# Reordering a block-triangular inverse in a recurrent layer: products formed at eviction, and one product pair moved a stage earlier

## The chip, the core and the metric

The kernel runs on one NeuronCore of one Trainium2 chip, as one program with float32 inputs and outputs. The metric is the device time in microseconds (us). The core has TensorE (PE, with its weight loads shown as PEld), VectorE (DVE), ScalarE (ACT), GpSimd (POOL) and SyncE (SP), which run side by side and meet at semaphores.

## The reference

A batch of 256 tokens of width 1024 goes through two blocks. The first has two layers; each layer is an MLP, a mixing stage, a cross attention to 256 memory tokens and a second MLP. The second block has a gated recurrence, a differential attention and a mixture of experts. The part that this case touches is the recurrent half of the mixing stage, with 8 heads of width 64. Per head and token it does

```
sa    = state @ (-kk_t)
state = state * w_t + outer(sa, b_t) + outer(v_t, k_t)
y_t   = state @ r_t
```

with `kk` normalised per head, `b = kk * a`, and a decay `w` per channel. After it come a norm per head, a bonus term and a gate. The cross attention then reads `rms_norm(mem)`, the memory tokens scaled by their inverse root mean square and by a gain.

## The kernel before

Every stage is a block of the program in which each engine has its own list, written out by hand, and all engines meet at a barrier at the end of each stage. Large matrix products stream weights from HBM in 1 MB chunks through a ring of five slots (SP issues them). ACT rounds each chunk (L264), DVE subtracts the rounded part (L274), and TensorE multiplies in three passes (L289 to L291).

`mix_in_stage` computes the projections, a local attention and the operands of the recurrence. Its last DVE instructions on those operands are L993 to L998: L998 makes the removal operand `a` (which lives in `b.removal`). After that DVE and ACT still mix the last projected columns (L905, L1009, L914) while TensorE ends with the last attention value product (L844).

`rwkv_stage` (L1111), called once per layer, does the recurrence in chunks of 64 tokens. There are four chunks, held as two token tiles t = 0, 1 of 128 partitions with two chunks each (`cp`), and eight heads `e`. Each pair of chunk and head is a 64 x 64 problem on one quadrant of the TensorE array (rows by the partition half of the operands, columns by the half of the result). A float32 product is recorded as two weight loads and two matmuls. The work, in TensorE's order:

- gate product L1358 into banks 6 and 7; then the chunk products L1369: 32 with the removal operand `Bb` into banks 0 to 3, and 32 with the key operand `Kb` into banks 4 to 7. DVE makes `Kb` (L1228) and masks all of them into `chunk_products`, called `m4` (L1232 for removal, L1244 for keys). ACT evicts the gate (L1321).
- The inverse X of a unit lower triangular matrix is built by doubling in six levels. POOL masks the part A of level `lv` (L1295, two instructions a level, one per token tile, into two buffers `AL`). Level 0 is L1401 and L1404, evicted by DVE as I minus the product (L1237 to L1239).
- Levels 1 to 5 each do: A X on TensorE (`level_ax`, L1412) -> ACT copies it to G (L1334) -> X^T G (L1421) and G^T X^T (L1426) -> DVE subtracts them from X (L1252) and from X^T (L1255). X and X^T are both kept, since each is the weight operand of one product. L1412 and L1421 use all four quadrants; L1426 uses two. Level 5 needs only X^T.
- Between A X and the updates, TensorE has filler work: transposes of v (level 1), of the read operand (2), of `Bb` (3), the product `bv` (L1435, level 4) and the transposes of `Kb` (5), evicted by ACT (L1328, L1340).
- The tail: X applied to the right sides (L1462, evicted negated by ACT L1346 and DVE L1258), then products that build state and read matrices (L1475, L1480, L1484, L1488), outputs (L1495, L1499), two state steps (L1517), the reads from the states (L1508) and the bonus sum (L1527).
- As soon as L1462 is done, POOL loads the 1 MB of memory tokens into `h` (L1306), waits for them, and scales them in two halves (L1311, L1313) for the next stage.

`memory_stage` follows the barrier and starts with ACT L264 and L2251.

## Time and profile before

| what | value |
|---|---|
| median of 3 runs | 2081.26 us (2078.82 to 2083.69) |
| the profiled execution's own time | 2080.44 us |
| its span in the profile | 2078.6 us |
| PE busy | 1991.8 us, 96% of the span |
| `rwkv_stage`, first layer | 329.3 to about 396.2 us |
| `rwkv_stage`, second layer | 1038.6 to about 1102.7 us |

The profiled execution took 1.8 us more than its span, and 0.8 us less than the median. The page gives busy time per engine; a timeline row is start, duration, engine, source line, operation, result<-operands, shape and count, with the idle time before it and what ended it in brackets.

### The profile page before, as it was taken

How to read it: one execution, taken by the hardware profiler on the slowest of the kernel's cores; microseconds unless marked ns; L12 is line 12 of the kernel's file. 1: busy time of each engine (PE TensorE's matmuls, PEld its weight loads, DVE VectorE, ACT ScalarE, POOL GpSimd, SP SyncE). 2: the span in 40 equal slices, each digit the busy share in tenths (PEclk: the TensorE clock that was granted, in tenths of full speed). 3: DMA queues.
4: the chain of work that ended last, by engine and by line, in shares of the span. 5: the costliest groups of instructions: out<-in, count | busy, mean ns of one | idle time of the engine just before them, and what ended most of it. 6: DMA issues, size and time to landing. Idle time of an engine off the chain costs nothing. (4 is left out here: it accounts for less than half of the span.)

```text
span 2078.6 us, 34505 instructions
## 1 busy us (share of the span) xinstructions
PE 1991.8 (96%) x14152; PEld 1734.2 (83%) x14152; DVE 1434.1 (69%) x1856; ACT 1084.2 (52%) x1639; POOL 346.1 (17%) x193
## 2 busy tenths in 40 slices
PE   6999998899999999999989999998999989999999
PEld 5888887799888878889878998887899987888887
DVE  5784765566677567656645756765686658999997
ACT  5444662454544454446524544444565547777775
POOL 1660004200065026400051003620000000000000
PEclk9999999999999999999999999998999989999999
DMA  9654430253565456534204536654433317999995
GB/s 361 255 223 170 147 117 3 87 186 136 222 237 209 142 216 248 211 144 160 75 24 145 181 114 251 243 191 101 163 122 122 133 67 293 368 372 371 371 372 192
DMA packets 56247, 402.47 MB, mean 194 GB/s; under 512 B 6360, under 2 KB 6544, under 8 KB 7840
## 3 DMA queue, kind: packets, MB, share of 16 engines
q1 hardware_dynamic: 51216, 368.64, 47.2%
q0 software_dynamic: 4880, 31.68, 4.5%
q8 instruction: 112, 1.84, 0.4%
q14 instruction: 39, 0.32, 0.0%
HBM read 399.23 MB, written 1.06 MB: 193 GB/s over the span
## 5 line engine op out<-in xcount | busy, mean ns | idle before, releaser
L274 DVE TENSOR_TENSOR weights_lo<-ring,weights_hi 128x1024 fp32r<-128x1024 f32 x696 | 928.6, 1377 | 178.5 <-ACT weights_hi L264 178.1
L264 ACT CAST weights_hi<-ring 128x1024 fp32r<-128x1024 f32 x696 | 694.6, 1050 | 247.4 <-PE ps L291 218.0
L289 PE MATMUL ps<-weights_hi,act_hi 128*128 128x512 f32 (+1 forms) x960 | 358.4, 373 | 22.2 <-DVE weights_lo L274 17.1
L290 PE MATMUL ps<-weights_lo,act_hi 128*128 128x512 f32 (+1 forms) x960 | 351.9, 367 | 0.0
L291 PE MATMUL ps<-weights_hi,act_lo 128*128 128x512 f32 (+1 forms) x960 | 351.7, 366 | 0.0
L289 PE MATMUL ps<-act_hi,weights_hi 128*128 128x256 f32 x992 | 295.7, 298 | 11.9 <-DVE act_lo L2340 6.3
L290 PE MATMUL ps<-act_lo,weights_hi 128*128 128x256 f32 x992 | 287.5, 290 | 0.0
L291 PE MATMUL ps<-act_hi,weights_lo 128*128 128x256 f32 x992 | 287.1, 289 | 0.0
L289 PEld LDWEIGHTS ps<-weights_hi,act_hi 128*128 128x128 f32 x960 | 182.1, 190 | 54.5 <-DVE weights_lo L274 17.1
L289 PEld LDWEIGHTS ps<-act_hi,weights_hi 128*128 128x128 f32 x992 | 196.9, 198 | 17.9 <-issue 10.3
L291 PEld LDWEIGHTS ps<-weights_hi,act_lo 128*128 128x128 f32 x960 | 182.0, 190 | 32.6
L290 PEld LDWEIGHTS ps<-weights_lo,act_hi 128*128 128x128 f32 x960 | 182.3, 190 | 30.0
L290 PEld LDWEIGHTS ps<-act_lo,weights_hi 128*128 128x128 f32 x992 | 197.4, 199 | 0.1
L291 PEld LDWEIGHTS ps<-act_hi,weights_lo 128*128 128x128 f32 x992 | 196.7, 198 | 0.0
L289 PE MATMUL ps<-weights_hi,slot_hi 128*128 128x512 f32 x320 | 128.3, 401 | 0.9 <-DVE weights_lo L274 0.9
L291 PE MATMUL ps<-weights_hi,slot_lo 128*128 128x512 f32 x320 | 125.4, 392 | 0.0
L289 PE MATMUL ps<-weights_hi,mlp_hidden_hi 128*128 128x512 f32 x320 | 125.3, 392 | 0.0
L291 PE MATMUL ps<-weights_hi,mlp_hidden_lo 128*128 128x512 f32 x320 | 125.0, 391 | 0.0
L290 PE MATMUL ps<-weights_lo,slot_hi 128*128 128x512 f32 x320 | 124.9, 390 | 0.0
L662 POOL TENSOR_TENSOR stretch<-stretch,params 128x2048 f32<-128x2048 f32 x24 | 86.5, 3603 | 230.0 <-PE ps L291 230.0
L290 PE MATMUL ps<-weights_lo,mlp_hidden_hi 128*128 128x512 f32 x320 | 124.4, 389 | 0.0
L460 ACT ACTIVATE stretch<-ps,norm_rs 128x256 f32<-128x256 f32 x88 | 37.0, 471 | 133.3 <-PE ps L291 133.3
(535 smaller groups left out, 3098.3 us busy)
## 6 DMA issues: line engine op xcount, KB each, us to landing
ring<-stream SPq DMA_DIRECT2D x348, 1024.0 KB, 4.9
stretch<-ada_in POOLq DMA_DIRECT2D x24, 1024.0 KB, 5.4
h<-mem_in POOLq DMA_DIRECT2D x2, 1024.0 KB, 5.2
consts<-w_consts SPq DMA_DIRECT2D x1, 1376.0 KB, 7.7
x<-x_in SPq DMA_DIRECT2D x1, 1024.0 KB, 4.9
stretch<-mem_in POOLq DMA_DIRECT2D x1, 1024.0 KB, 10.1
bias_t<-bias_scratch POOLq DMA_DIRECT2D x1, 1024.0 KB, 6.8
out<-x SPq DMA_DIRECT2D x4, 256.0 KB, 2.1
```

Source lines behind the costliest of these rows:

```text
L264: core.nc.scalar.copy(self.hi[:, self.place(i), part], core.slot(chunk)[:, part]).then_inc(self.rounded.sem, 1)
L274: core.nc.vector.tensor_tensor(self.lo[:, self.place(i), part], core.slot(chunk)[:, part], self.hi[:, self.place(i), part].bitcast(F32), A ...
L289: nc.tensor.matmul(out, lhs[0], rhs[0], start=start, stop=False, **kw)
L290: nc.tensor.matmul(out, lhs[0], rhs[1], start=False, stop=False, **kw)
L291: return nc.tensor.matmul(out, lhs[1], rhs[0], start=False, stop=stop, **kw)
L460: nc.scalar.activation(sg[:, j % 2, t, :], inner_bank(j, t)[:, 0:STEP], ACT.Silu, scale=acts.rs[:, t:t + 1]).then_inc(silu.sem, 1)
L662: nc.gpsimd.tensor_tensor(w, w, c.unsqueeze(2).to_broadcast([P, KB, STEP]), ALU.mult).then_inc(self.added.sem, 1)
```

## The change

Only the recurrence and what feeds it are changed; the mathematics is the same.

- The 32 removal products move from the start of `rwkv_stage` to the end of TensorE's list in `mix_in_stage`. They wait for L998 (`removed`) and go to banks 2, 3, 6 and 7. The core's first DVE work is now their masking.
- G is no longer A X but I - A X: DVE forms it when it evicts the bank (`factor`), in place of ACT's copy. With that G, both updates are plain products, X G and its transpose, and are copied out, not subtracted from the old X. ACT copies X of tile 0 and the whole of X^T (both tiles, two banks, one instruction; only tile 0 in level 5), DVE copies X of tile 1 (and X^T of tile 1 in level 5).
- The turned update goes to all four quadrants: the layout of G and X^T over banks and halves changes with the level (`crosses`, `factor_place`, `end_place`).
- TensorE's list in a level is now A X of tile 0, filler, A X of tile 1, filler, then the X updates, then both turned updates. The fillers are: the key products in levels 1 and 2, the read transposes in 3, the `Bb` transposes in 4, `bv` in 5. The transposes of v go ahead of level 0 (banks 4, 5), and those of `Kb` between level 5 and the product with the right sides.
- POOL masks levels 0 and 1 first, and weighs `Bb` after level 3 and `Kb` after level 5.
- The memory is loaded in two halves of 512 KB. The second is issued when the first has landed, ahead of the scaling of the first.

```diff
+    removed = core.sig("removal_ready", 1)
+    b.removal_products = core.sig("removal_products_ready", TT)
...
+            pe.wait_ge(removed.sem, removed.at(1))
+            for t in range(TT):
+                ins = chunk_products(core, level_bank(t), a, b.read, t)
+                ins.then_inc(b.removal_products.sem, 1)
...
+                    stt(a[:, :, :], a[:, :, :], 0.5, L[:, :, :], ALU.mult, ALU.mult).then_inc(removed.sem, 1)
...
+def level_bank(t):
+    return 6 if t else 2
+
+
+def chunk_products(core, bank, w, reads, t):
+    for q in range(4):
+        for flip in range(2):
+            for cp in range(2):
+                hd = (flip + cp) % 2
+                own, rows = slice(64 * cp, 64 * cp + 64), slice(64 * hd, 64 * hd + 64)
+                tokens = slice((2 * t + cp) * CHUNK, (2 * t + cp + 1) * CHUNK)
+                ins = core.nc.tensor.matmul(core.ps[own, bank + hd, q * P:(q + 1) * P].rearrange("p (i n) -> p i n", i=2),
+                                            w[rows, q, tokens], reads[rows, :, q, tokens], start=True, stop=True)
+    return ins
...
+        TURN, UPDATE = 0, 4
+
+        def crosses(e, lv):
+            return (e & 1) ^ (e >> 1 & lv & 1)
...
+            def mask_removal(t):
+                dve.wait_ge(b.removal_products.sem, b.removal_products.at(t + 1))
+                for j in range(2):
+                    tt(m4[:, t, 4 * j:4 * j + 4, A_T:P_T + 1, :].rearrange("p e i n -> p e (i n)"),
+                       ps[:, level_bank(t) + j, :].rearrange("p (e n) -> p e n", e=4),
+                       tri.unsqueeze(1).to_broadcast([P, 4, P]), ALU.mult).then_inc(masked_b.sem, 1)
+
+            def mask_keys(t):
+                dve.wait_ge(prod.sem, prod.at(t + 1))
+                for j in range(2):
+                    tt(m4[:, t, 4 * j:4 * j + 4, B_T:Q_T + 1, :].rearrange("p e i n -> p e (i n)"),
+                       ps[:, TURN + j, :].rearrange("p (e n) -> p e n", e=4),
+                       tri.unsqueeze(1).to_broadcast([P, 4, P]), ALU.mult).then_inc(masked_k.sem, 1)
+
+            def first_inverse(t):
+                dve.wait_ge(gdone.sem, gdone.at(t + 1))
+                for w in range(2):
+                    tt(turned_first[:, w, t, :, 1, :], over_heads(ident64)[:, 0:2],
+                       bank4(level_bank(t) + 1).rearrange("p (d w) n -> p w d n", w=2)[:, w], ALU.subtract)
+                tt(X[:, t], over_heads(ident64), bank8(level_bank(t)), ALU.subtract).then_inc(x_v.sem, 1)
+
+            def first_turned(t):
+                for w in range(2):
+                    ins = tt(turned_first[:, w, t, :, 0, :], over_heads(ident64)[:, 0:2],
+                             AL[0][:, t].rearrange("p (d w a) n -> p w a d n", w=2, a=2)[:, w, 0], ALU.subtract)
+                ins.then_inc(xt_first.sem, 1)
+
+            def factor(lv, t):
+                dve.wait_ge(gdone.sem, gdone.at(lv * TT + t + 1))
+                tt(in_banks(G[:, t]), ident64.unsqueeze(1).unsqueeze(1).to_broadcast([P, 2, 4, 64]), level_banks(t),
+                   ALU.subtract).then_inc(g_in.sem, 1)
+
+            for t in range(TT):
...
+                    factor(lv, t)
+                    if lv == 1:
+                        first_turned(t)
+                if lv < levels - 1:
+                    dve.wait_ge(pdone.sem, pdone.at((lv - 1) * TT + 2))
+                    nc.vector.tensor_copy(in_banks(X[:, 1]), level_banks(1)).then_inc(x_v.sem, 1)
+                if lv <= TT:
+                    mask_keys(lv - 1)
+            dve.wait_ge(tdone.sem, tdone.at(levels - 1))
+            nc.vector.tensor_copy(XT[:, 1].rearrange("p t s n -> p (t s n)"), ps[:, UPDATE + 1, :]).then_inc(xt_v.sem, 1)
...
+            mask_level(0)
+            mask_level(1)
+            for c in (1, 2):
+                ins = tt(diag[:, c - 1], ident64.unsqueeze(1).to_broadcast([P, 4, 64]), last(c), ALU.mult)
+            mask_level(2)
+            mask_level(3)
+            weigh_to_end(Bb).then_inc(late.sem, 1)
+            mask_level(4)
+            mask_level(5)
+            pool.wait_ge(prod.sem, prod.at(TT))
+            weigh_to_end(Kb).then_inc(late.sem, 1)
...
-            nc.gpsimd.dma_start(h[:, :, :], b.mem_in).then_inc(mem_loaded.sem, 16)
-            pool.wait_ge(mem_loaded.sem, mem_loaded.at(16))
...
+            nc.gpsimd.dma_start(h[:, 0:4, :], b.mem_in[:, 0:4, :]).then_inc(mem_loaded.sem, 16)
             for i in range(2):
                 part = h[:, 4 * i:4 * i + 4, :]
+                pool.wait_ge(mem_loaded.sem, mem_loaded.at(16 * (i + 1)))
+                if i == 0:
+                    nc.gpsimd.dma_start(h[:, 4:8, :], b.mem_in[:, 4:8, :]).then_inc(mem_loaded.sem, 16)
...
+                if lv < levels - 1:
+                    act.wait_ge(pdone.sem, pdone.at((lv - 1) * TT + 1))
+                    nc.scalar.copy(in_banks(X[:, 0]), level_banks(0)).then_inc(x_s.sem, 1)
+                act.wait_ge(tdone.sem, tdone.at(lv))
+                if lv < levels - 1:
+                    ins = nc.scalar.copy(work[:, 1, :], ps[:, UPDATE:UPDATE + 2, :].rearrange("p w n -> p (w n)"))
                 else:
-                    take_turned(3)
+                    ins = nc.scalar.copy(XT[:, 0].rearrange("p t s n -> p (t s n)"), ps[:, UPDATE, :])
+                ins.then_inc(xt_s.sem, 1)
...
+            def level_products(lv, t):
+                pe.wait_ge(g_in.sem, g_in.at((lv - 1) * TT + t + 1))
+                if lv == 1:
+                    pe.wait_ge(xt_first.sem, xt_first.at(t + 1))
+                else:
+                    pe.wait_ge(xt_s.sem, xt_s.at(lv - 1))
+                for e, cp in quarters():
+                    f = crosses(e, lv - 1)
+                    ins = mm(level_banks(t)[half(cp), f, e // 2, :], xt(half(cp ^ f), t, e),
+                             G[half(cp ^ f), t, factor_place(e, lv - 1), :], start=True, stop=True)
+                ins.then_inc(pdone.sem, 1)
...
+            def level_turned(lv, t):
+                if lv == 1:
+                    pe.wait_ge(moved.sem, moved.at(TT))
+                elif lv == levels - 1:
+                    pe.wait_ge(g_in.sem, g_in.at((lv - 1) * TT + t + 1))
+                    pe.wait_ge(xt_s.sem, xt_s.at(lv - 1))
+                for e, cp in quarters((0, 2, 1, 3, 4, 6, 5, 7)):
+                    f, f_next, w, s = crosses(e, lv - 1), crosses(e, lv), e >> 1 & 1, 2 * (e >> 2) + (e & 1)
+                    at = t * 256 + s * 64
+                    ins = mm(ps[half(cp ^ f_next), UPDATE + w, at:at + 64], G[half(cp ^ f), t, factor_place(e, lv - 1), :],
+                             xt(half(cp ^ f), t, e), start=True, stop=True)
+                if t == TT - 1:
+                    ins.then_inc(tdone.sem, 1)
...
+            for t in range(TT):
+                transposed(0, v_, t, UPDATE)
             for t in range(TT):
                 first_level(t)
             for lv in range(1, levels):
+                level_ax(lv, 0)
+                if lv == 3:
+                    pe.wait_ge(masked_k.sem, masked_k.at(2 * TT))
+                    transposed(1, qr[:, 0], 0)
+                elif lv == 4:
+                    pe.wait_ge(moved.sem, moved.at(2 * TT))
+                    pe.wait_ge(late.sem, late.at(1))
+                    transposed(2, Bb, 0)
+                elif lv == 5:
+                    pe.wait_ge(moved.sem, moved.at(3 * TT))
+                    bv(0)
+                level_ax(lv, 1)
+                if lv <= TT:
+                    key_products(lv - 1)
+                elif lv == 3:
+                    transposed(1, qr[:, 0], 1)
+                elif lv == 4:
+                    transposed(2, Bb, 1)
+                else:
+                    bv(1)
+                if lv < levels - 1:
+                    for t in range(TT):
+                        level_products(lv, t)
                 for t in range(TT):
-                    level_ax(lv, t)
-                if lv == 1:
-                    transposed(0, v_)
-                elif lv == 2:
-                    transposed(1, qr[:, 0])
-                elif lv == 3:
-                    pe.wait_ge(late.sem, late.at(1))
-                    transposed(2, Bb)
-                elif lv == 4:
-                    bv()
-                else:
-                    pe.wait_ge(late.sem, late.at(2))
-                    transposed(3, Kb)
-                for t in range(TT):
-                    level_products(lv, t)
-
+                    level_turned(lv, t)
```

## Rows read from the trace of the kernel before

**Rows 1.** The page: share of the engines, and the chain that ended last.
```profile
PE 1991.8 (96%) x14152; PEld 1734.2 (83%) x14152; DVE 1434.1 (69%) x1856; ACT 1084.2 (52%) x1639; POOL 346.1 (17%) x193
...
PE 18%; DVE 0%; ACT 0%; issue 0%; DVEq 0%; ACTq 0%
```

**Rows 2.** Busy time by stretch: engines, granted clock, DMA share, GB/s.
```profile
329.30:350.80 21.50, 17.64 (x405) 15.15 (x407) 12.38 (x18) 3.43 (x6) 13.03 (x13) 0.76 0.01 3
350.80:374.70 23.90, 21.13 (x814) 18.70 (x812) 9.41 (x15) 8.63 (x16) 13.41 (x12) 1.00 0.02 4
374.70:396.20 21.50, 17.17 (x466) 15.56 (x460) 5.95 (x12) 2.12 (x5) 9.02 (x5) 0.92 0.16 52
...
1038.60:1058.90 20.30, 16.39 (x407) 14.10 (x409) 12.05 (x18) 3.43 (x6) 12.51 (x13) 0.83 0.01 2
1058.90:1083.60 24.70, 21.64 (x827) 19.48 (x827) 9.55 (x16) 8.83 (x16) 13.89 (x12) 1.00 0.02 4
1083.60:1102.70 19.10, 15.36 (x453) 13.76 (x444) 5.95 (x12) 2.12 (x5) 9.02 (x5) 1.00 0.18 59
```

**Rows 3.** Timeline, first layer: mixing stage ends, core begins.
```profile
324.02 1.22 DVE L998 SCALAR_TENSOR_TENSOR stretch<-stretch 128x1024 f32<-128x1024 f32 x1
...
326.27 0.86 PE L844 MATMUL ps<-probs_T,y 128*64 128x256 f32 x4
...
328.04 0.88 DVE L914 SCALAR_TENSOR_TENSOR stretch<-unmixed,params,stretch 128x255 f32<-128x255 f32 x2 [0.97 <-ACT stretch L1009]
...
329.32 3.37 PE L1358 MATMUL ps<-stretch,gate_up 128*128 128x256 f32 x8 [2.19 <-PEq L746]
...
334.02 2.48 DVE L1232 TENSOR_TENSOR chunk_products<-ps,consts 128x512 f32<-128x512 f32 x4 [3.02 <-PE ps L1369]
...
334.65 1.92 PE L1369 MATMUL ps<-stretch,rwkv_work 64*64 64x128 f32 x64
335.39 4.95 POOL L1295 TENSOR_TENSOR rwkv_work<-chunk_products,consts 128x512 f32<-128x512 f32 x4 [3.91 <-DVE chunk_products L1232]
...
336.72 0.97 PE L1401 MATMUL ps<-consts,rwkv_work 64*64 64x64 f32 x26 [0.15 <-POOL rwkv_work L1295]
...
339.11 1.52 DVE L1239 TENSOR_TENSOR rwkv_work<-consts,rwkv_work 128x256 f32<-128x256 f32 x1
...
341.48 0.49 DVE L1239 TENSOR_TENSOR rwkv_work<-consts,rwkv_work 128x256 f32<-128x256 f32 x1
...
344.42 1.97 PE L1394 MATMUL ps<-consts,stretch 128*128 128x128 f32 x8 [2.02 <-DVE chunk_products L1244]
```

**Rows 4.** Timeline, first layer, second to fourth level.
```profile
350.91 1.10 PE L1412 MATMUL ps<-rwkv_work 64*64 64x64 f32 x62
...
351.62 1.07 ACT L1334 COPY y<-ps 128x512 f32<-128x512 f32 x2 [4.61 <-PE ps L1412]
...
354.97 1.04 PE L1426 MATMUL ps<-rwkv_work,y 64*64 64x64 f32 x30
...
366.67 0.38 PE L1435 MATMUL ps<-chunk_tokens,chunk_products 64*64 64x64 f32 x9 [1.72 <-issue]
...
370.23 0.50 PE L1426 MATMUL ps<-rwkv_work,y 64*64 64x64 f32 x9 [0.66 <-issue]
```

**Rows 5.** DMA traffic of the second stretch, 40 slices of 0.6 us.
```profile
GB/s 0 0 27 0 0 0 0 0 0 27 0 0 0 0 0 27 0 0 0 0 0 0 27 0 0 0 0 0 27 0 0 0 0 0 27 0 0 0 0 0
...
q8 instruction: 6, 0.10, 1.8%
```

**Rows 6.** Busy time by stretch between stalls of TensorE, first layer.
```profile
366.60:370.20 3.60, 2.90 (x127) 2.76 (x127) 1.98 (x3) 1.07 (x2) 2.96 (x2) 1.00 0.02 5
```

**Rows 7.** Timeline, both layers: the tail with the memory load.
```profile
377.25 0.59 POOL L1306 DMA_DIRECT2D h<-mem_in  x1 [7.60 <-PE ps L1462]
...
384.45 0.37 PE L1488 MATMUL ps<-chunk_products,rwkv_work 64*64 64x64 f32 x2 [3.74 <-issue]
...
1092.58 0.97 PE L1495 MATMUL ps<-chunk_tokens,chunk_products 64*64 64x64 f32 x26 [3.46 <-issue]
```

More of the change, by code:

```diff
@@ L1235, in _ @@
[L1235 to L1246 removed]
+                first_inverse(t)
@@ L1397, in first_level, with key_products @@
+            def key_products(t):
+                if t == 0:
+                    pe.wait_ge(right.sem, right.at(1))
+                    pe.wait_ge(gate.sem, gate.at(1))
+                else:
+                    pe.wait_ge(masked_k.sem, masked_k.at(2))
+                chunk_products(core, TURN, Kb, qr, t).then_inc(prod.sem, 1)
             def first_level(t):
                 pe.wait_ge(masked.sem, masked.at(t + 1))
[L1399 to L1402 removed]
+                for e, cp in quarters():
+                    mm(ps[half(cp), level_bank(t), e * 64:(e + 1) * 64], AL[0][half(cp), t, e, :], ident64[half(cp), :],
+                       start=True, stop=True)
@@ L1439, in _, with bv @@
+            def bv(t):
+                for e, cp in quarters():
+                    f, at = crosses(e, levels - 1), t * 256 + end_place(e) % 4 * 64
+                    ins = mm(ps[half(cp ^ f), TURN + f, at:at + 64], m4[half(cp), t, e, B_T, :], v_tok[half(cp), t, e, :],
+                             start=True, stop=True)
+                if t == TT - 1:
+                    ins.then_inc(bv_done.sem, 1)
+            for t in range(TT):
+                transposed(0, v_, t, UPDATE)
             for t in range(TT):
@@ new lines, in _ @@
+            pe.wait_ge(bv_moved.sem, bv_moved.at(2))
+            pe.wait_ge(late.sem, late.at(2))
+            for t in range(TT):
+                transposed(3, Kb, t)
+            pe.wait_ge(xt_s.sem, xt_s.at(levels - 1))
+            pe.wait_ge(xt_v.sem, xt_v.at(1))
+            for t in range(TT):
+                for e, cp in quarters():
+                    f, at = crosses(e, levels - 1), end_place(e) % 4 * P
+                    ins = mm(ps[half(cp), level_bank(t) + f, at:at + P], xt(half(cp ^ f), t, e),
+                             KqBv[half(cp ^ f), t, end_place(e), :, :].rearrange("p i n -> p (i n)"), start=True, stop=True)
```

249 lines of the change are left out of this document (97 added, 152 removed).

## Prediction, made before the result was known

> **What bounds the kernel now.** I read the page first, then the stretches of the two recurrent stages, their timelines, and last the DMA traffic inside them. The page says that TensorE is busy for 96% of the span and that the chain that ended last is TensorE's products of the last stage [rows 1]. So a change to the recurrent core pays only by shortening its own 67 us and 64 us; these stages lie between barriers, and nearly no weights move in them (2 to 4 GB/s outside the memory load [rows 2]), so what they lose is not made up elsewhere and what they save passes on whole.
>
> I cut each core in three: A from the barrier to the A X of level 2, B from there to the product with the right sides, C the tail. They take 21.5, 23.9 and 21.5 us in the first layer, 20.3, 24.7 and 19.1 in the second [rows 2].
>
> A is a chain across engines. In it TensorE's records fill 17.6 of 21.5 us, but at a mean granted clock of 0.76 [rows 2]; gate and removal products come first, then DVE's masks at 334.0, POOL's at 335.4, level 0 at 336.7, and the transposes of v wait until 344.4 for DVE to finish the key masks [rows 3].
>
> B looks like a chain too, but the rows say otherwise. Groups of 64 passes on four quadrants take 1.1 us [rows 4], 128 recorded instructions, 8.6 ns each. Then TensorE stops in the middle of a group (L1435 with 9 passes left, L1426 with 9 left), where no semaphore stands, for 1.72 and 0.66 us, put down to "issue" [rows 4]. From one resumption to the next are 3.56 us [rows 4] and 127 + 127 records, some 256 instructions with a couple of waits [rows 6]. In that stretch the only DMA traffic is six packets of the instruction queue, 0.10 MB, so 16 KB each, and they come 6 or 7 slices of 0.6 us apart, 3.6 to 4.2 us [rows 5]. I read this as code loading: TensorE gets its next 256 instructions no sooner than about 3.6 us after entering the present ones, 14 ns per instruction, while four quadrants eat one in 8.6 ns. B has 804 passes, 1608 instructions; at 14 ns that is 22.5 us of its 23.9 and 24.7. B is already at the rate at which code arrives.
>
> The Trainium skill (Advanced Engine Details and Errata, ISA Cache) describes a cache of two lines of 256 instructions each; the trace agrees, with stops some 256 instructions apart. Its page Runtime: NRT & Kernel Launch (Instruction fetch mechanics) says the fetch is hidden behind instruction issue; the trace shows stops of 0.66 to 1.72 us instead. Taken at its word, that page would give the first rival below.
>
> C holds the largest single stop: 3.74 us in L1488 in the first layer, 3.46 us in L1495 in the second, both "issue", both after the 1 MB load was issued at 377.25 (first layer) [rows 7]. A code packet queued behind that load fits; stops without a load are 0.66 to 1.72 [rows 4], so the load adds some 2 to 3.
>
> **End of the mixing stage.** The removal operand is ready at 324.02 + 1.22 = 325.2, before TensorE ends its values at 327.1, so the new wait costs nothing; nothing is queued behind it but the moved products. These are 64 passes of 1.92 us [rows 3] and a switch of shape, so they end at about 329.3. They hide behind DVE's last mixing, which ends at 328.92 [rows 3]. Past it they stick out 0.4 us: **+0.4 per layer**. Without that cover it would be 2.
>
> **Part A after, in us from the barrier.** DVE masks two of four at 1.24 (2.48 for four), POOL's first mask takes 1.24 (4.95 for four), ready at 2.6 [rows 3]. TensorE needs longer: gate 3.4 at the low clock of that moment, eight transposes of v 1.1 to 2.0 (1.97 at the low clock [rows 3]), so 4.5; level 0 is 1.2 per tile (0.97 + 0.26 to the last of it) [rows 3], done at 7.0. DVE's first inverse is one 512-column instruction at 0.6 and two short ones, 1.3 together, done at 8.5. Then DVE carries level 1: factor 0.62, first turned part 0.5, both for each tile: 10.8. Factor is the kind of L1232 (PSUM and a constant), 0.62 each. The first turned part is the kind of L1239, whose same instruction took 0.49 once and 1.52 while POOL was at a mask [rows 3]; it comes as two short instructions a tile, POOL is busy with masks and the diagonal then, so between 0 and 4 blocked of up to 1.0 each; I take 1.5 in all, nearest to the one of two blocked rows: 12.3. The X and turned products of the last tile take 0.6 + 1.1 with their latencies: 14.3. I take **14.5**; 13 with no blocking and no low clock, 17 with all four blocked or another low stretch. Against 21.5 and 20.3: **-7.0 and -5.8**. The key masks (2 x 0.62 a tile) stand behind DVE's X copies and are covered by A X and the key products. Code does not bind A: 312 passes, 624 instructions, 9 us.
>
> The Trainium skill (SBUF — State Buffer, SBUF: two separate sides) has it that a DVE instruction with two SBUF inputs waits out a whole GpSimd instruction that reads SBUF. It speaks against the change, as more of those pairs meet here; by the row 1.03 is lost each time, by the rule up to the 1.24 of a mask.
>
> **Part B after.** By dependencies alone a level would be short: both X updates 1.1, both turned updates 1.1 (now at L1412's 1.1 per 64 passes and not L1426's 1.04 per 30 [rows 4]), ACT's copy of X^T 1.05 (1.07 for the same 1024 columns in two instructions [rows 4]) with 0.35 of latencies, 3.7 us. Four quadrants for the turned product save 0.5 per 32 passes, 4 us over levels 2 to 5, and DVE's in-place subtracts leave the chain. But no instruction is gone: 320 passes of A X, 256 and 320 of the updates are as many as before. The list from level 2 to the right sides even grows from 804 to 836 passes, by the 32 of the second key products; the other fillers only shift inside it. At the rate of code, 24.3 (mean of both layers) x 836 / 804 = 25.3: **+1.0 per layer**. Bounds: 18, if only dependencies and quadrants count (below), and 28 with a stretch at the low clock (a 3.4 us stretch costs 1.7 of work) and dependencies adding to stops. ACT's and DVE's shorter work costs and gives nothing here.
>
> **Part C after.** Same products. Two half loads let a code packet in between: a packet now waits for at most half the traffic, or meets neither. Of the 2 to 3 us I take 1.9 back, bounds 0.5 and 3.7. In the first layer the low clock came right after the stop (granted 0.92 over 21.5 us, against 1.00 over 19.1 [rows 2]); a chance of its going adds 0.4: **-2.3 per layer**. POOL waits for one half, scales it while the other lands, and ends before TensorE does; it is later by an issue of 0.59 [rows 7], covered by the outputs.
>
> **Sum**, against the profiled execution: first layer +0.4 - 7.0 + 1.0 - 2.3 = -7.9, second +0.4 - 5.8 + 1.0 - 2.3 = -6.7, together -14.6: 2080.4 - 14.6 = 2065.8, and for the median, 0.8 above the profiled one, 2066.6. I say 2066.
>
> **Rivals.**
> - *Code does not bind the levels.* If the stops are something that the new order avoids, B takes 18 us, not 25.3, and C another 1 less: 2066 - 2 x 8.3 = 2049. Against it: stops inside groups with no semaphore and the even packets; for it: only two stops of B are printed as such. 16%.
> - *Blocking on DVE's port, and DVE as the bound.* All short turned parts blocked, factor and X copies late behind the key masks: A is 17.5, B 26.5, so 2066 + 2 x 4.2 = 2074. 10%.
> - *The gain is eaten within 0.2%.* DVE's blocking as above, and the half loads each catch a packet, so that C gives nothing: 2074 + 4.6 = 2079. 6%.
> - *Clock, the other side.* TensorE now stops every 256 instructions. If the chip grants the low level for it, each 3.4 us costs 1.7 us of work. It decides from 9 such stretches over both layers; at 11, most of both B parts, the time is 2085. Against it: B ran at 1.00 in both layers with the same stops [rows 2]. 5%.
>
> **How the numbers follow.** The forecast has 63%, its own range is 2058 to 2072 (A 1.5, B 1.5, C 1.2 per layer to either side). The range of 2050 to 2076 takes in about half of the first rival and all of the second, and leaves out the rest of the first and the last two, some 19%. Within 0.2% (4.2 us) is about what this measurement can't tell from no change. Faster 0.87, same 0.08, slower 0.05.
>
> **What would show it.** Right: L1401 begins some 4.5 us after the barrier and not 7.4; A X of level 2 at 14 to 15; in B stops put down to "issue" in most levels, code packets every 3.6 to 3.9 us, the same number of passes; in C two loads of half the size and a stop under 2 us. Wrong if B falls under 22 us (code was not the limit), if L1239's successors take over 1 us each, or if the granted clock in B falls below 0.95.

## The result, and the profile after

The changed kernel takes 2064.99 us (median of 4 runs, 2063.95 to 2066.41) against 2080.11 us for the kernel before on the same chip: a ratio of 0.9925, 95% interval 0.9908 to 0.9942. The forecast was 2066, with the range 2050 to 2076. The profiled execution has a span of 2062.2 us, 16.4 under the one before.

The page of the changed kernel, its line on TensorE, which answers to the first of [rows 1]: as many passes, 16.8 us less busy time.

```profile
PE 1975.0 (96%) x14152; PEld 1718.8 (83%) x14152; DVE 1429.0 (69%) x1858; ACT 1086.6 (53%) x1637; POOL 346.3 (17%) x195
```

Busy time by stretch after, cut as in [rows 2]: A, B and C of the first layer, then of the second. The columns are the stretch, its length, busy time and count of PE, PEld, DVE, ACT and POOL, granted clock, DMA share, GB/s.

```profile
329.80:341.96 12.16, 9.66 (x309) 8.39 (x313) 9.60 (x19) 2.64 (x5) 9.92 (x9) 1.00 0.01 3
341.96:367.11 25.15, 19.00 (x853) 16.55 (x844) 10.61 (x17) 10.12 (x15) 16.04 (x16) 1.00 0.02 5
367.11:386.10 18.99, 15.46 (x457) 14.08 (x456) 5.26 (x11) 2.86 (x7) 9.57 (x6) 1.00 0.19 59
1030.20:1042.70 12.50, 9.90 (x313) 8.49 (x317) 10.04 (x19) 2.64 (x5) 10.28 (x9) 1.00 0.01 3
1042.70:1068.75 26.05, 19.01 (x851) 16.54 (x839) 10.11 (x16) 10.13 (x15) 15.70 (x16) 1.00 0.02 5
1068.75:1088.80 20.05, 17.04 (x457) 15.57 (x456) 5.26 (x11) 2.86 (x7) 9.58 (x6) 0.91 0.18 56
```

| part | first layer, before to after | forecast | second layer, before to after | forecast |
|---|---|---|---|---|
| A | 21.5 to 12.16: -9.3 | -7.0 | 20.3 to 12.50: -7.8 | -5.8 |
| B | 23.9 to 25.15: +1.3 | +1.0 | 24.7 to 26.05: +1.4 | +1.0 |
| C | 21.5 to 18.99: -2.5 | -2.3 | 19.1 to 20.05: +1.0 | -2.3 |

The cores make 131.0 us before and 114.9 after: -16.1 of the 16.4. A alone gives 17.1; B costs 2.6, where 2.0 was forecast; C gives in the one layer and loses in the other. A's granted clock, 0.76 and 0.83 in [rows 2], is now 1.00 in both layers.

The timeline of the first layer after: the end of the mixing stage and part A, which answers to [rows 3].

```profile
327.36 1.98 PE L1128 MATMUL ps<-stretch 64*64 64x128 f32 x64
...
328.35 0.88 DVE L920 SCALAR_TENSOR_TENSOR stretch<-unmixed,params,stretch 128x255 f32<-128x255 f32 x2 [0.98 <-ACT stretch L1015]
...
329.81 1.97 PE L1439 MATMUL ps<-stretch,gate_up 128*128 128x256 f32 x8 [0.47 <-PEq L748]
...
332.58 0.97 PE L1467 MATMUL ps<-consts,rwkv_work 64*64 64x64 f32 x26
...
334.71 0.97 PE L1467 MATMUL ps<-consts,rwkv_work 64*64 64x64 f32 x26 [0.73 <-POOL rwkv_work L1356]
...
336.58 0.68 DVE L1289 TENSOR_TENSOR rwkv_work<-consts,ps 128x512 f32<-128x512 f32 x1
...
339.15 1.18 DVE L1293 TENSOR_TENSOR rwkv_work<-consts,rwkv_work 128x128 f32<-128x128 f32 x2
```

The gate product (L1439) took 3.37 us in [rows 3] and takes 1.97 at the same 8 passes. Level 0 begins 2.8 us after the barrier at 329.81. The inverse of level 0 is complete (second tile, L1289) at 7.5, the last of the first turned parts (L1293) at 10.5, and A X of level 2 begins at 12.15.

TensorE's stops in B of the first layer, which answer to the stops of [rows 4]; each row is what it resumes with.

```profile
344.45 0.35 PE L1484 MATMUL ps<-rwkv_work 64*64 64x64 f32 x9 [1.44 <-issue]
...
347.75 0.85 PE L1509 MATMUL ps<-rwkv_work,y 64*64 64x64 f32 x42 [0.80 <-issue]
...
354.98 0.69 PE L1484 MATMUL ps<-rwkv_work 64*64 64x64 f32 x32 [1.04 <-issue]
...
358.68 0.38 PE L1496 MATMUL ps<-y,rwkv_work 64*64 64x64 f32 x9 [0.24 <-issue]
...
362.06 0.39 PE L1517 MATMUL ps<-chunk_tokens,chunk_products 64*64 64x64 f32 x10 [1.24 <-issue]
...
365.71 0.45 PE L1509 MATMUL ps<-rwkv_work,y 64*64 64x64 f32 x12 [1.39 <-issue]
```

They stand some 3.5 us apart (344.45 to 365.71 are six steps, one of them without a stop), and sum to 6.15 us. Busy time and stops together are the 25.15 us of B: TensorE waits for nothing else there. Its busy time in B fell from 21.13 to 19.00 us and the stretch grew all the same, so the saved work became stops. The DMA traffic of that stretch, as in [rows 5]: seven packets of code, five or six slices of 0.63 us apart, and nothing else.

```profile
GB/s 26 0 0 0 0 26 0 0 0 0 26 0 0 0 0 0 26 0 0 0 0 0 26 0 0 0 0 0 26 0 0 0 0 26 0 0 0 0 0 0
...
q8 instruction: 7, 0.11, 1.8%
```

The trace also says when each packet of this queue (q8) sets out. After the resumption at 344.45 none does until 345.57; the traffic of 344.45:345.67 holds the next one:

```profile
q8 instruction: 1, 0.02, 4.9%
```

TensorE resumes 2.2 us after it, at 347.75. This holds for every stop put down to "issue" in the two recurrent stages from 338 and 1038 us on, in the traces of all fourteen kernels: 197 stops of 0.15 to 4.91 us, each of which ends 2.1 to 3.0 us after the latest code packet set out. And no packet set out less than 1.03 us after such a resumption. So a stop ends when code has come, and the 3.5 us from one to the next are some 1.1 to the packet and 2.4 from it to the resumption.

The tail after, which answers to [rows 7]: both issues of the memory load, and the two stops of TensorE around the first.

```profile
369.43 0.59 POOL L1375 DMA_DIRECT2D h<-mem_in  x1 [10.63 <-PE ps L1562]
...
370.39 0.33 PE L1575 MATMUL ps<-chunk_tokens 64*64 64x64 f32 x4 [0.39 <-issue]
...
374.26 0.53 POOL L1380 DMA_DIRECT2D h<-mem_in  x1 [4.23 <-DMA h<-mem_in]
...
375.86 0.27 PE L1588 MATMUL ps<-chunk_products,rwkv_work 64*64 64x64 f32 x2 [2.92 <-issue]
...
1077.16 1.16 PE L1595 MATMUL ps<-chunk_tokens,chunk_products 64*64 64x64 f32 x28 [2.63 <-issue]
```

The stop is 2.92 us, where the forecast had it under 2 (3.74 before). In the second layer, the last row, it is 2.63 (3.46 before). The transfers of the first half run from 370.72 to 373.46 us, in the second layer to 1075.00, and the code packet that ends the stop sets out at 373.46 and at 1075.01: it came when that half was through.

### The profile page after: what moved, and what is told of

It reads as the page before. It is cut to its first block and busy times, and to the rows that moved or that the text cites. A ratio compares the mean times of both kernels' runs of the same rounds, so it can differ in the third digit from the quotient of the medians.

```text
span 2062.2 us, 34473 instructions
## 1 busy us (share of the span) xinstructions
PE 1975.0 (96%) x14152; PEld 1718.8 (83%) x14152; DVE 1429.0 (69%) x1858; ACT 1086.6 (53%) x1637; POOL 346.3 (17%) x195
## 5 line engine op out<-in xcount | busy, mean ns | idle before, releaser
L289 PE MATMUL ps<-weights_hi,act_hi 128*128 128x512 f32 (+1 forms) x960 | 358.3, 373 | 22.1 <-DVE weights_lo L274 17.1
L289 PEld LDWEIGHTS ps<-weights_hi,act_hi 128*128 128x128 f32 x960 | 182.1, 190 | 54.5 <-DVE weights_lo L274 17.1
```

Source lines behind the costliest of these rows:

```text
L289: nc.tensor.matmul(out, lhs[0], rhs[0], start=start, stop=False, **kw)
```

## The experiments

Twelve kernels ran. Unless it is said otherwise each is the changed kernel with one edit, and times are medians. The changed kernel was measured beside the kernel before at 2080.11 us, e1 to e4 beside it at 2081.06, e5 to e8 at 2080.26, and the last four at 2079.01.

| kernel | us | runs | ratio to before, 95% |
|---|---|---|---|
| e1 two quadrants | 2066.2 | 4 | 0.9923 (0.9906 to 0.9940) |
| e2 writes in levels | 2065.48 | 1 | |
| e3 no memory load | 2062.4 | 1 | |
| e4 whole load | 2070.65 | 4 | 0.9943 (0.9927 to 0.9960) |
| e5 removal products in the core | 2069.59 | 4 | 0.9942 (0.9922 to 0.9962) |
| e6 before, with warming products | 2075.07 | 10 | 0.9978 (0.9969 to 0.9988) |
| e7 before, with two halves | 2080.18 | 10 | 0.9994 (0.9984 to 1.0004) |
| e8 both halves later | 2056.32 | 4 | 0.9892 (0.9870 to 0.9913) |
| e9 long writes | 2069.53 | 1 | |
| e10 changed kernel again | 2061.42 | 5 | 0.9911 (0.9897 to 0.9925) |
| e11 both halves later, again | 2059.67 | 6 | 0.9911 (0.9897 to 0.9925) |
| e12 whole load later | 2061.27 | 4 | 0.9912 (0.9895 to 0.9928) |

### Does code bind B? e1

The turned update goes over the heads in an order that keeps two quadrants busy at a time; nothing else is changed.

```diff
-                for e, cp in quarters((0, 2, 1, 3, 4, 6, 5, 7)):
+                for e, cp in quarters((0, 1, 4, 5, 2, 3, 6, 7)):
```

> The changed kernel with one edit: the turned update walks the heads in the order 0, 1, 4, 5, 2, 3, 6, 7, so that neighbouring products use only two of the four quadrants. Nothing else, the same output. My theory (levels 2 to 5 wait for TensorE's code, some 3.6 to 3.7 us per 256 instructions): the turned groups take 1.04 us per 32 passes and not 0.58, but the stretch from A X of level 2 to the right sides stays at 25 to 26.5 us in both layers, and the whole is within 3 us of the changed kernel's 2065. Rival (TensorE's array time and the quadrants made or limit this stretch): 8 groups of 32 passes by 0.46 give +3.7 us there and +4.6 with level 1, so +9 us over both layers, 2074.

Measured: 2066.2 us, 1.2 above the changed kernel's 2064.99, with intervals that overlap. By groups of line and operation in B of the first layer, first the changed kernel, columns: count, busy time, mean of one in ns, idle time before them and what ended it:

```profile
L1509 PE MATMUL ps<-rwkv_work,y 64*64 64x64 f32 x272 | 5.7, 220 | 2.2 <-issue 2.2
```

and the same group with two quadrants:

```profile
L1509 PE MATMUL ps<-rwkv_work,y 64*64 64x64 f32 x274 | 7.3, 223 | 2.7 <-issue 2.7
```

And B of this kernel, by stretch, in both layers:

```profile
341.85:368.88 27.03, 20.59 (x855) 18.14 (x846) 10.38 (x16) 10.12 (x15) 15.86 (x16) 1.00 0.02 4
...
1042.88:1069.33 26.45, 20.90 (x854) 18.47 (x845) 9.94 (x15) 10.14 (x15) 15.46 (x16) 1.00 0.02 4
```

The products do run longer, 20.6 and 20.9 us in B against 19.0 to 19.4, and B takes 27.0 and 26.5 us, the first 0.5 above what was expected. With its code untouched B takes 25.0 to 28.3 us, 26.4 in the mean, over the two layers of the changed kernel and of e3, e4, e8, e10, e11 and e12. The rival's +9 us is out. But the edit lengthened the products by less than half of the 3.7 us that the rival had counted on. Had all of it come through, the kernel would be some 3.5 us longer, and two medians with such intervals can't exclude that. What speaks for the theory is the stops: they sum to 6.4 and 5.6 us where 7.3 is the mean of the untouched kernels, and stand in the same places of the list, 3.9 and 3.8 us apart on average (3.5 to 4.0 in the two traces of the changed kernel). So e1 fits a hidden price and does not prove it; that code binds B rests on the packets above and on e9.

### Do code packets wait behind other traffic? e2 and e9

In e2 SyncE writes x, 1 MB, to scratch memory at the start of levels 2 and 4; nothing reads it.

```diff
+            for i, lv in enumerate((2, 4)):
+                sp.wait_ge(gdone.sem, gdone.at(lv * TT + 1))
+                sp.dma_start(b.extra[i], b.x[:, :, :]).then_inc(extra_loaded.sem, 16)
```

> The changed kernel, and in addition SyncE writes 1 MB from SBUF to an unused place in HBM twice in each core, issued when A X of level 2 and of level 4 (tile 0) is done. No engine waits for these writes in the levels, and no operand comes from them. Theory (TensorE's stops are code that has not arrived, and other DMA traffic delays it): the code packets that meet a write come late, so there are two stops of 2 to 4 us in place of 1 to 1.5 us, and the stretch from A X of level 2 to the right sides grows by 3 to 6 us per layer. Rival (the stops come from the engine itself or from a wait between engines): the stretch stays within 0.5 us.

Measured: 2065.48 us in one run, B 27.4 and 26.9. That missed the expectation; at most 1 us a layer over the mean of B can be seen. The stops show that the writes did not hold a packet for long: the one after the first write is 1.62 us against 0.80 in the changed kernel, in the second layer 1.60 against 1.33, and e12 has 1.62 in that place with no write at all. A write lasts about as long as the way from one packet to the next, and here it had nearly ended when the packet was due. That made the run inconclusive, and e9 puts four such writes one after the other, so that no packet can miss them.

```diff
+            sp.wait_ge(gdone.sem, gdone.at(2 * TT + 1))
+            for i in range(4):
+                sp.dma_start(b.extra[i], b.x[:, :, :]).then_inc(extra_loaded.sem, 16)
```

> The changed kernel, in which SyncE writes 4 MB (four times the 1 MB of the stream x, to scratch memory that nothing reads) one after the other from the start of level 2 on; the outputs don't depend on it. One writing of 1 MB takes 2.8 to 4.1 us here, so the four cover some 12 to 16 us of part B, more than the 3.6 us from one code packet to the next, and this time a packet can't miss them. Theory (code packets wait behind other traffic of the same engines, which is what makes the stop of part C): TensorE's stops in part B grow, by the row of part C to some 3 us for each packet that is asked for behind a queue of writes; B takes 30 to 36 us in place of 25 to 27, the kernel 8 to 20 us more than the changed one. Rival (the stop of part C has another cause, for instance that the load reads the chip's memory through the queue of GpSimd): B 25 to 27.5 us and the time within 3 us of the changed kernel's 2065.

Measured: 2069.53 us in one run. Its timeline: the first two stops of B in the first layer, and the long one in the second, with its counterpart in the changed kernel below:

```profile
341.93 0.35 PE L1492 MATMUL ps<-rwkv_work 64*64 64x64 f32 x9 [1.27 <-issue]
...
349.35 1.44 PE L1517 MATMUL ps<-rwkv_work,y 64*64 64x64 f32 x42 [4.91 <-issue]
...
1053.71 1.13 PE L1517 MATMUL ps<-rwkv_work,y 64*64 64x64 f32 x32 [4.89 <-issue]
```

```profile
1049.37 0.69 PE L1509 MATMUL ps<-rwkv_work,y 64*64 64x64 f32 x32 [1.33 <-issue]
```

The traffic of e9 from the resumption at 341.93 to 346.94, all of it the writes' queue, and the code packet that is there when the window ends at 347.04:

```profile
q1 hardware_dynamic: 281, 2.05, 100.3%
```

```profile
q8 instruction: 1, 0.02, 1.1%
```

B by stretch, both layers:

```profile
339.59:369.44 29.85, 21.17 (x855) 18.35 (x845) 10.64 (x17) 10.11 (x15) 16.15 (x16) 0.89 0.36 144
...
1043.66:1075.38 31.72, 22.44 (x855) 19.21 (x848) 10.51 (x17) 10.13 (x15) 16.08 (x16) 0.84 0.34 136
```

In the first layer it is the same stop as in the changed kernel (L1509 there), with the same 42 passes left of its group: 4.91 us where it was 0.80. In the second layer it is 4.89 us where it was 1.33. Only SyncE got anything to do, and its transfers touch no semaphore that TensorE waits for. The stop is 3.6 to 4.1 us longer. The packet that ends it sets out 5.0 us after the resumption in both layers, where the changed kernel has 1.1 and 1.3, with the writes' queue busy all the while; TensorE resumes 2.4 us after it, as ever. So it is the packet that comes late. B is 3.5 and 5.3 us above its mean of 26.4. A part of that is the clock, 0.89 and 0.84 over these B and 1.00 over all the others; the low stretch of the first layer begins about with the end of the stop:

```profile
349.30:356.20 6.90, 6.86 (x131) 5.28 (x133) 1.37 (x2) 1.60 (x2) 2.79 (x3) 0.54 0.32 129
```

The kernel as a whole is 4.5 us above the one median of the changed kernel and 8 above the other, so at or under the low end of the 8 to 20 that the theory expected: in each layer one packet came late enough to show, and not several. The rival (nothing) is out.

### The load and the tail: e3, e4, e7, e8

e3 leaves out the memory load, so that cross attention works on other numbers.

> The changed kernel without the load of the memory tokens; GpSimd scales what lies in the buffer, so the cross attention gets other numbers. Theory: the stop in L1588 or L1595, 2.92 and 2.63 us after the change, falls to 0.5 to 1.5 us, what code alone costs there, and the tail shortens by 1.5 to 2 us per layer. Rival (the load does not touch TensorE): the stop stays at 2.6 to 2.9.

Measured: 2062.4 us in one run. C, by stretch, first layer:

```profile
366.95:384.61 17.66, 15.47 (x457) 14.09 (x456) 5.26 (x11) 2.87 (x7) 8.45 (x4) 1.00 0.02 4
```

With no load the stop is 1.00 us in the place where the changed kernel has 2.92, and 1.26 for 2.63 in the second layer, as the theory had it; C takes 17.7 and 17.5 us. So the load as the change places it still costs C 1.3 us in the one layer and 2.6 in the other.

e4 undoes the halves: one load of 1 MB at the place of the first half.

```diff
-            nc.gpsimd.dma_start(h[:, 0:4, :], b.mem_in[:, 0:4, :]).then_inc(mem_loaded.sem, 16)
+            nc.gpsimd.dma_start(h[:, :, :], b.mem_in).then_inc(mem_loaded.sem, 16)
```

> The changed kernel with the memory loaded in one piece again. Theory: the stop goes from 2.9 and 2.6 us back to about 3.7 and 3.5, so +0.8 us per layer, +1.7 in all, near the bound of what can be told. Rival (as I predicted, the halves carry 1.9 us per layer): +1.9 per layer, +3.8 in all.

Measured: 2070.65 us, 5.7 over the changed kernel, more than the theory (1.7) and the rival (3.8); the two ratios have intervals that overlap. The stop is 3.47 and 3.18 us in place of 2.92 and 2.63, C is 20.9 and 22.3 us. Only 0.6 us a layer of it is the stop. The granted clock of C was 0.92 and 0.85, against 1.00 and 0.91 in the changed kernel. B, which the edit does not touch, was 1.6 and 1.5 us longer as well.

e7 is the kernel before with the two halves alone.

> The kernel before with the memory loaded in two halves, nothing else. Theory: the stop of 3.7 and 3.5 us in the tail shrinks by 0.5 to 1 us per layer, -1 to -2 us in all. Rival (predicted): -1.9 per layer, -3.8 in all.

Measured: 2080.18 us over 10 runs, ratio 0.9994 (0.9984 to 1.0004): nothing, so the theory's -1 to -2 us isn't seen and the predicted -3.8 is out. Its stop is 2.64 us in the first layer (3.74 in [rows 7]) and 3.46 in the second, as before; C 19.9 and 20.8 us against 21.5 and 19.1. So the halves took 1.1 us from one stop and nothing from the other, and C moved by more than that both ways.

e8 keeps the halves and asks for the first one product later.

```diff
-            pool.wait_ge(gh_done.sem, gh_done.at(2))
+            pool.wait_ge(mt_done.sem, mt_done.at(1))
```

> The changed kernel with the first half load issued when the state matrices are done (some 1.9 us later) instead of when the right sides are done. Theory: the code packet that came 5.4 us after the one before it gets in ahead of the load, so the stop in L1588 or L1595 falls from 2.9 and 2.6 to about 1 to 1.5 us; the half loads then meet a later packet, where TensorE has waits of its own to hide it. GpSimd ends 1.9 us later, still ahead of TensorE by about 1 us. -1 to -1.5 us per layer, 2062 to 2064. Rival (the load delays the next packet by as much, and TensorE stops there): no change within 1 us, or GpSimd ends last and the stage gets 0.5 us longer.

Measured: 2056.32 us (2054.64 to 2062.49), 8.7 under the changed kernel, where 1 to 3 were expected. The stop fell to 1.00 and 0.98 us, as expected. C is 17.4 and 17.2 us, as short as without a load (e3). That is 1.6 and 2.9 us; 3 us more lie ahead of the first core, which began at 326.8 and not 329.8, and nothing of the edit acts there in the first layer. (In e11, the same kernel measured again, the first core begins at 326.85, in all the others at 327.5 or later. What sets it is open.)

### Is the gain of A the chain or the clock? e5 and e6

e5 puts the removal products back to the start of the core.

> The changed kernel with the removal products back at the head of the core (TensorE's first work there), all else as changed. The products themselves take 1.9 us; DVE's masks, GpSimd's and level 0 stand behind them. Theory (moving them gave A its shorter chain and, by keeping TensorE at work at the end of the mixing stage, the high granted clock): the chain to level 0 grows by about 2 us, the stage before ends 0.5 us earlier, and the granted clock falls to the low level in the first 4 us again, costing up to 1.7 us more: +1.5 to +3.5 us per layer, 2068 to 2072. Rival (the gain of A came from the levels' new form alone): within 1 us of 2065.

Measured: 2069.59 us, 4.6 over the changed kernel; the intervals of the ratios overlap, but part A shows the difference by itself. From the first removal product to A X of level 2 in both layers, and then the stretch of the low clock in the first:

```profile
328.53:343.26 14.73, 12.96 (x369) 11.49 (x373) 9.33 (x18) 2.64 (x5) 10.17 (x9) 0.88 0.01 3
...
1030.85:1045.83 14.98, 13.04 (x371) 11.37 (x374) 9.99 (x20) 2.64 (x5) 10.66 (x9) 0.89 0.01 3
```

```profile
329.10:332.50 3.40, 3.40 (x58) 3.04 (x53) 1.66 (x3) 0.00 (x0) 0.71 (x1) 0.55 0.04 10
```

A is 2.6 and 2.5 us longer. The 64 passes take 3.55 us here and 1.98 at the end of the mixing stage. Before them TensorE had idled for 2.18 us while DVE ended the mixing, and for 3.4 us from 329.1 the clock was granted at 0.55: nearly all of that stretch at 1.2 GHz and not 2.4. The theory held. Seen from the kernel before, the new order without the move takes A from 21.5 and 20.3 us to 14.7 and 15.0, and the move to 12.2 and 12.5.

e6 takes the other side: the kernel before, and at the end of its mixing stage the 64 passes of the removal products as well, into banks that nobody reads. They are work too much; all the rest of the change is absent.

```diff
+            pe.wait_ge(removed.sem, removed.at(1))
+            for t in range(TT):
...
+                            mm(ps[own, (6 if t else 2) + hd, q * P:(q + 1) * P].rearrange("p (i n) -> p i n", i=2),
+                               a[rows, q, tokens], b.read[rows, :, q, tokens], start=True, stop=True)
```

> The kernel before, with one addition: TensorE does the removal products a second time at the end of the mixing stage (64 passes, 1.9 us) into banks that nobody reads, behind the same wait as in the changed kernel. The core is the old one. Theory (the low granted clock at the head of the core, 3.4 us from 329.9, comes from TensorE's idle time ahead of it): the granted clock stays high there, the stage before ends 0.4 us later, the gate product takes 2.0 us and not 3.4, net -1 us per layer, 2077 to 2079. Rival (the clock has nothing to do with it): +0.4 us per layer and the same low stretch.

Measured: 2075.07 us over 10 runs, ratio 0.9978 (0.9969 to 0.9988), 5.2 us under the kernel before, more than the 1 to 3 that the theory expected. Its timeline at the start of the core, then A by stretch in both layers:

```profile
326.98 1.98 PE L901 MATMUL ps<-stretch 64*64 64x128 f32 x64
329.40 1.96 PE L1369 MATMUL ps<-stretch,gate_up 128*128 128x256 f32 x8 [0.44 <-PEq L747]
```

```profile
329.37:348.17 18.80, 15.11 (x407) 13.24 (x409) 12.05 (x18) 3.44 (x6) 12.51 (x13) 0.91 0.01 3
...
1032.62:1051.43 18.81, 14.94 (x406) 13.09 (x407) 12.05 (x18) 3.44 (x6) 12.51 (x13) 0.91 0.01 3
```

The products cost nothing where they stand, since DVE still mixes. The idle time ahead of the gate product falls from 2.19 us [rows 3] to 0.44, the gate product runs in 1.96 and not 3.37, and A's granted clock is 0.91 and not 0.76. A falls from 21.5 and 20.3 us to 18.8 in both, 4.2 us together. The rest of the 5.2 isn't in A. The 128 added instructions also move the places where code ends: the whole load, issued at the same point of the program, now meets a stop of 1.70 us in the first layer and one of 4.00 in the second, for 3.74 and 3.46, and C takes 17.8 and 21.0 us, for 21.5 and 19.1. So of A's gain of 9.3 and 7.8 us, 2.7 and 1.5 come from filling that idle time with anything at all; the other 6.6 and 6.3, from 18.8 to 12.2 and 12.5, need the new order (and hold the low stretch that the old order still has in its later waits: 0.91 to 1.00). No run undoes the parts of that order one by one (G formed at the eviction, the fillers between the tiles, POOL's masks first), so what each of them gives is not shown.

### How much is the later load worth? e10, e11, e12

The changed kernel again, e8's kernel again, and e4 with its one load at the later place, on one chip.

> The changed kernel as it is, timed beside the next two. 2065 us, 15 us under the kernel before; it is the measure for the two others.

> The version with both half loads asked for one product later (after the state's product mt instead of after gh), again, beside the changed kernel on the same chip. Theory (the code packet that TensorE asks for right after gh was caught behind the first half, and is now ahead of it): 2.5 us less in each layer's tail, so 5 us under the changed kernel, 2060; the 8.7 us seen the first time also held some 3 us that lay ahead of the first core and may not come again. Rival (all of the first gain was chance of the run): within 2 us of the changed kernel.

> The same later place, but one load of 1 MB, not two halves. If only the meeting with the code packet counts, the halves are worth nothing here: the time is that of the two halves at the later place, within 2 us. If the halves have a worth of their own (GpSimd scales one while the other lands, and the next packet finds a shorter queue), it is 3 to 6 us longer, as it was at the earlier place (5.7 us).

Measured: 2061.42 us (2057.87 to 2066.36), 2059.67 (2057.65 to 2063.49) and 2061.27 (2058.34 to 2063.64). By the medians the later load gains 1.7 us, and its ratio to the kernel before has the same interval as the changed kernel's. The rival of e11 (within 2 us) took this one. Of e12's two answers the first came true: with the later place the whole load is within 2 us of the halves. The two measurements of the changed kernel, 2064.99 and 2061.42, differ by more than that, so a step of under 4 us can't be told from one comparison.

The traces do repeat, in the stop and in C. e11, first layer, the issue of the first half and the stops around it:

```profile
367.73 0.33 PE L1575 MATMUL ps<-chunk_tokens 64*64 64x64 f32 x4 [0.39 <-issue]
...
368.89 0.59 POOL L1375 DMA_DIRECT2D h<-mem_in  x1 [13.28 <-PE ps L1580]
...
371.28 0.27 PE L1588 MATMUL ps<-chunk_products,rwkv_work 64*64 64x64 f32 x2 [1.00 <-issue]
```

and e12, with the whole load:

```profile
372.43 0.33 PE L1574 MATMUL ps<-chunk_tokens 64*64 64x64 f32 x4 [0.39 <-issue]
...
373.58 0.59 POOL L1375 DMA_DIRECT2D h<-mem_in  x1 [14.38 <-PE ps L1579]
...
375.98 0.27 PE L1587 MATMUL ps<-chunk_products,rwkv_work 64*64 64x64 f32 x2 [1.00 <-issue]
```

In both the load is issued 1.2 us after TensorE resumes at one stop, and the next comes 3.55 us on, with 1.00 us of rest. In the changed kernel it is issued 1.0 us before (369.43 against 370.39), and the next resumption is 5.47 us on. A load's first transfer comes 1.3 us after its issue in all three, while the code packet sets out at 368.95 (e11) and 373.65 (e12), so ahead of the load's transfers, and in the changed kernel behind them. So behind the packet the size of the load does not count: C of e12 is 17.1 and 17.0 us, of e11 17.1 and 17.7, of e10 19.0 and 21.5. Ahead of it the load costs a stop of 3.47 and 3.18 us whole (e4), and of 1.82 to 3.01 by halves (both layers of the changed kernel, e1, e2, e5, e9 and e10). By C alone the later place is worth some 2 us in the first layer and 2 to 3 in the second. (In e10 the difference there is 3.8, but 1.4 of it is L1562 at the low clock, ahead of the load.) The medians show 8.7 us in one comparison and 1.7 in the other. The traces of the second pair don't stand for its medians: e10's is of its longest execution, 2066.36 us, and e11's of one at 2057.92, so that the two traces differ by 8.4 us. What makes one execution longer is open; B alone varies by up to 3.3 us with the same code (in e10 25.0 and 28.3), which is as large as what is looked for.

## Why the prediction was right, point by point

- **Code binds B: shown.** Every stop ends 2.1 to 3.0 us after a code packet set out, and ends later when the packet does (e9). The list grew and B with it, by 1.3 and 1.4 us where +1.0 was forecast; the seven kernels above give B a mean of 26.4, and the kernels with the old order (before, e6, e7) one of 24.2, so +2.2 is the fairer size. TensorE's 2.1 to 2.6 us less of work and DVE's in-place subtracts off the chain gave nothing that shows. The rival at 2049, "Code does not bind the levels", is out. The Trainium skill (Advanced Engine Details and Errata, ISA Cache) has two lines of 256 instructions. The stops, 3.5 us and some 256 instructions apart, agree with the length of a line; no run here shows how many there are. The Trainium skill's page Runtime: NRT & Kernel Launch (Instruction fetch mechanics) has the fetch hidden, and stops of 0.24 to 1.44 us in B say otherwise.
- **Part A: right in its mechanism, too small.** The sum had 14.5 us after, 13 at the least; 12.2 and 12.5 came. By its steps: level 0 starts at 2.8 and not 4.5, since gate and transposes ran at full clock (1.97 and 1.04 us and not 3.4 and up to 2.0). It then waits 0.73 for POOL's mask, and is done at 6.3 for 7.0. The first inverse is at 7.5 for 8.5, the turned parts at 10.5 for 12.3: of the four short instructions the first of each pair waited for POOL, 0.37 and 0.70 us, where the sum had put 1.5 of blocking. The term that was left out was the clock: the forecast took the low clock at the head of the core as given, and moving the removal products takes it away (e5, e6).
- **DVE's port: it blocks, but is not the bound.** Timeline rows of both engines after:

```profile
337.66 0.61 POOL L1362 TENSOR_TENSOR rwkv_work<-consts,chunk_decay 128x256 f32<-128x256 f32 x1
337.77 0.65 DVE L1293 TENSOR_TENSOR rwkv_work<-consts,rwkv_work 128x128 f32<-128x128 f32 x1
...
338.71 1.27 POOL L1356 TENSOR_TENSOR rwkv_work<-chunk_products,consts 128x512 f32<-128x512 f32 x1 [0.43 <-DVE rwkv_work L1293]
...
339.15 0.98 DVE L1293 TENSOR_TENSOR rwkv_work<-consts,rwkv_work 128x128 f32<-128x128 f32 x1
```

  Twice DVE's short instruction starts inside one of POOL's and ends 0.15 us after it: 338.42 against 338.27, and 340.13 against 339.98. The other of each pair took 0.28 (the shortest of this line), so that 1.07 us were lost, and not the 4 x 1.0 of the rival at 2074, which is out. The Trainium skill (SBUF — State Buffer, SBUF: two separate sides) has a DVE instruction with two SBUF inputs wait out a whole GpSimd instruction; here the trace agrees, and the price is what was left of POOL's instruction.
- **Part C: the step that was mis-sized.** "I take 1.9 back" of the stop; it fell by 0.8 in each layer (3.74 to 2.92, 3.46 to 2.63), and by e4 the halves made 0.6 of that in each. The mechanism held, a code packet behind the load: in the kernel before, the changed kernel, e1, e4, e5, e6 and e10 it sets out between 0.3 us before and 0.2 us after the load's last transfer. e9 shows such waiting too, and in e3, e8, e11 and e12 the stop is down to 1.0 to 1.3 us, with the load gone or issued after the resumption. What was wrong is the price of a half: its transfers took 2.3 to 2.8 us in these kernels and those of the whole load 3.5 to 3.7, so that half the bytes save about a third of the time at best. The clock did the rest: the low stretch left C of the first layer and came to C of the second (1.00 to 0.91). The forecast had -4.6 over both layers, the profile shows -1.5; A's surplus of 4.3 more than covered that.
- **End of the mixing stage: right.** The products end at 327.36 + 1.98 = 329.34, DVE's last mixing at 329.23: 0.1 us out for 0.4.
- **The clock, other side: not in B, but once behind it.** B was granted 1.00 in both layers with all its stops, as forecast, and in every kernel but e9, where a stop of 4.9 us is followed by the low level and B is at 0.89 and 0.84. No stop so long is needed: in e10, the same program as the changed kernel, B of the second layer ends with stops of 1.8, 0.7, 1.8 and 1.9 us, and 0.4 us into C the clock goes down for 3.4 us. L1562 takes 3.39 us there and 1.98 elsewhere, so this rival is real at the price of one stretch.

```profile
1070.10:1073.50 3.40, 3.40 (x80) 3.40 (x74) 0.99 (x2) 1.28 (x3) 0.04 (x1) 0.50 0.02 5
```

That two sizes were off by 3 to 4 us in opposite directions, and the sum only by 1, is partly luck. The same program at its second measurement (e10, 2061.42 us) is 4.6 us under the forecast. (The forecast's own sum was 2066.6, written as 2066.)

## What to carry to other kernels

If TensorE stops in the middle of a group with nothing to wait for, at even steps of 256 instructions, count instructions, not passes or quadrants: less work per instruction gave nothing here. That fewer instructions would help follows from this, but no run tried it. A load in such a stretch should be issued after TensorE has passed a stop, not just ahead of it; its size matters less. Look at what TensorE does in the last microseconds ahead of a chain: work that is moved into that idle time pays twice, by its own length and by the clock, and even useless products there shortened this kernel, by 4.2 us in the stretch behind them.

## What the runs showed of the hardware

- With products that nobody reads the kernel before was 5.2 us faster (e6), 4.2 of it in part A: TensorE came to the core after 0.44 us of rest and not 2.19, and was granted the 2.4 GHz level there.
- A stop for code ends 2.1 to 3.0 us after the code packet (16 KB, 256 instructions) set out, and the packet sets out 1.0 us or more after the resumption before it; that held for 197 stops in fourteen traces.
- A code packet that met the memory load set out when the load was through (within 0.3 us), and half a load took 2.3 to 2.8 us, a whole one 3.5 to 3.7.
- Code packets come late behind writes of another queue to other memory: one set out 5.0 us after the resumption and not 1.1 or 1.3, and a stop of 0.8 or 1.3 us became 4.9 (e9).
- The same list of TensorE gives B from 25.0 to 28.3 us; the places of the stops don't move, their lengths do. What sets them from one time to the next is open.
